# Gate and up weights of an expert in four transfers instead of two, in a hybrid decoder layer with 32 experts

## The reference

```python
def _hier_moe(x, w_r1, b_r1, w_r2, b_r2, w_gate, w_up, w_down):
    # top-1 of 4 groups, then top-2 of the 8 experts in the group; gate = p_group * p_expert
    ...
    for g in range(N_EXPERT_GROUPS):
        hg = jnp.einsum('nd,edf->nef', x, w_gate[g])
        hu = jnp.einsum('nd,edf->nef', x, w_up[g])
        a = jax.nn.silu(hg) * hu * gate[:, g, :, None].astype(x.dtype)
        y = y + jnp.einsum('nef,efd->nd', a, w_down[g]).astype(jnp.float32)
    return y.astype(x.dtype)
```

## Time and profile before

| | |
|---|---|
| median of three runs | 1018.94 us |
| profiled execution | 1017.82 us, of which span 1016.0 us |
| TensorE matmul busy | 906.7 us (89%) |
| TensorE weight load | 641.8 us (63%) |
| VectorE | 554.0 us (55%) |
| ScalarE | 409.7 us (40%) |
| GpSimd | 131.2 us (13%) |
| DMA, whole span | 273.49 MB, mean 269 GB/s |
| granted TensorE clock, mean | 0.958 |

### The profile page before, as it was taken

One profiled execution on the slowest core, in us unless ns is written; L12 is line 12 of the kernel. 1 busy time (PEld: TensorE's weight loads), 2 busy tenths in 40 slices (PEclk: granted clock), 3 DMA queues, 4 the chain that ended last, 5 costly groups with the idle time before them and its releaser, 6 DMA issues.

```text
span 1016.0 us, 13340 instructions
## 1 busy us (share of the span) xinstructions
PE 906.7 (89%) x5132; PEld 641.8 (63%) x5132; DVE 554.0 (55%) x1023; ACT 409.7 (40%) x748; POOL 131.2 (13%) x83
## 2 busy tenths in 40 slices
PE   6999999986999999759999826999999999999585
PEld 6999879953555545438888525666666666666231
DVE  5202020048566575683544476767676767666057
ACT  5202020034554644571222231564656555555045
POOL 0000000130000000000000002345464311111100
PEclk9999999988999999999999857999999999999888
DMA  9999999299587676418722373899999999995464
GB/s 349 310 366 357 353 346 345 76 395 251 184 319 246 232 249 208 166 36 322 248 83 68 135 325 104 308 366 362 369 350 358 350 373 354 366 355 198 161 254 167
DMA packets 54847, 273.49 MB, mean 269 GB/s; under 512 B 13984, under 2 KB 16544, under 8 KB 39680
## 3 DMA queue, kind: packets, MB, share of 16 engines
q1 hardware_dynamic: 46016, 247.97, 68.1%
q0 software_dynamic: 8768, 24.66, 6.9%
HBM read 256.33 MB, written 95.30 MB: 346 GB/s over the span
## 4 chain that ended last, share of the span: by engine, by line
PE 77%; DVE 10%; DMA 7%; issue 3%; ACT 3%; SPq 0%; POOLq 0%; DVEq 0%; ACTq 0%
PE psum L645 69%; DMA back<-w_gu 4%; PE psum L704 4%; PE psum L883 2%; DVE back L1231 1%; DMA back<-pair_d 1%; ACT back L490 1%; DVE back L1213 1%; DVE stats L1216 1%; PE psum L843 1%; ACT back L995 1%; DMA middle<-pair_d 1%; PE psum L906 1%; DVE middle L1241 1%; DVE middle L1590 0%
## 5 line engine op out<-in xcount | busy, mean ns | idle before, releaser
L645 PE MATMUL psum<-back,front 128*64 128x128 f32 (+1 forms) x896 | 147.9, 356 | 8.0 <-ACT back L490 4.4
L645 PEld LDWEIGHTS psum<-back,front 128*64 128x64 f32 (+1 forms) x896 | 69.4, 147 | 63.8 <-issue 54.3
L1656 POOL DMA_INDIRECT pair_d<-front,back x32 | 79.6, 2487 | 205.8 <-ACT front L1106 124.6
L645 PE MATMUL psum<-gu_high,xg_high 128*112 128x512 f32 x256 | 104.1, 407 | 2.1 <-DVE xg_low L1481 2.1
L645 PE MATMUL psum<-front 64*128 64x256 f32 (+5 forms) x384 | 92.6, 500 | 10.5 <-DVE stats L1213 9.9
L645 PE MATMUL psum<-gu_high,xg_low 128*112 128x512 f32 x256 | 101.8, 398 | 0.0
L645 PE MATMUL psum<-gu_low,xg_high 128*112 128x512 f32 x256 | 101.6, 397 | 0.0
L645 PE MATMUL psum<-x_high,w_high 128*128 128x352 f32 x288 | 93.7, 325 | 8.2 <-DVE w_low L361 8.2
L645 PE MATMUL psum<-x_low,w_high 128*128 128x352 f32 x288 | 93.0, 323 | 0.0
L645 PE MATMUL psum<-x_high,w_low 128*128 128x352 f32 x288 | 92.9, 322 | 0.0
L490 ACT COPY back<-psum 128x512 f32<-128x512 f32 (+1 forms) x88 | 46.9, 547 | 87.1 <-PE psum L704 86.9
(11 more groups left out here) (199 smaller groups left out, 1635.0 us busy)
## 6 DMA issues: line engine op xcount, KB each, us to landing
out_win_k_s<-cache_win_k SPq DMA_DIRECT2D x16, 2044.0 KB, 13.8
out_win_v_s<-cache_win_v SPq DMA_DIRECT2D x16, 2044.0 KB, 12.6
back<-w_down SPq DMA_DIRECT2D x24, 1024.0 KB, 14.7
front<-w_gu SPq DMA_DIRECT2D x22, 1024.0 KB, 12.7
middle<-w_gu SPq DMA_DIRECT2D x22, 1024.0 KB, 13.1
back<-w_gu SPq DMA_DIRECT2D x20, 1024.0 KB, 15.3
back<-winkT SPq DMA_DIRECT2D x8, 1792.0 KB, 8.0
back<-cache_win_v SPq DMA_DIRECT2D x8, 1024.0 KB, 7.5
```

The lines of the kernel that those rows point to most:

```text
L645: return nc.tensor.matmul(out, lhsT, rhs, start=start, stop=stop, skip_group_check=True)
L1656: G.indirect_dma_start(pair_d, bass.IndirectOffsetOnAxis(ap=IDX[0:CAP, NE + e:NE + e + 1], axis=0), YS[e % 2][0:CAP, :], None, bounds_chec ...
```

## The change

The gate and up weights of an expert are loaded in four transfers of 512 KB, two k-tiles each, in place of two of 1 MB. Each quarter has its own semaphore, ScalarE waits before each of its four casts, and TensorE signals `s_gu` after every second k-tile, so that SyncE is given back each quarter by itself. The other waits on `s_gu` count in quarters. Sizes and places of the buffers, the order on each engine and the bytes that are moved stay the same.

```diff
-        s_gf = [[sem(f"s_gf{i}_{h}") for h in range(2)] for i in range(3)]
+        s_gf = [[sem(f"s_gf{i}_{q}") for q in range(4)] for i in range(3)]
...
-        def load_gu(sp, e, half):
-            k = slice(4 * half, 4 * half + 4)
-            sp.dma_start(GUF[e % 3][:, k, :], I["w_gu"][e][:, k, :]).then_inc(s_gf[e % 3][half], 16)
+        def load_gu(sp, e, q):
+            k = slice(2 * q, 2 * q + 2)
+            sp.dma_start(GUF[e % 3][:, k, :], I["w_gu"][e][:, k, :]).then_inc(s_gf[e % 3][q], 16)
...
-            for half in range(2):
-                load_gu(sp, 0, half)
+            for q in range(4):
+                load_gu(sp, 0, q)
...
             for e in range(3, NE):
-                for half in range(2):
-                    sp.wait_ge(s_gu, 2 * (e - 3) + half + 1)
-                    load_gu(sp, e, half)
+                for q in range(4):
+                    sp.wait_ge(s_gu, 4 * (e - 3) + q + 1)
+                    load_gu(sp, e, q)
...
-                    if k % 4 == 3:
+                    if k % 2 == 1:
                         last.then_inc(s_gu, 1)
...
             def weights_rounded(e):
                 if e >= 2:
-                    act.wait_ge(s_gu, 2 * (e - 1))
+                    act.wait_ge(s_gu, 4 * (e - 1))
                 for q in range(4):
-                    if q % 2 == 0:
-                        act.wait_ge(s_gf[e % 3][q // 2], 16 * (e // 3 + 1))
+                    act.wait_ge(s_gf[e % 3][q], 16 * (e // 3 + 1))
                     k = slice(2 * q, 2 * q + 2)
                     nc.scalar.copy(GUH[e % 2][:, k, :], GUF[e % 3][:, k, :]).then_inc(s_wh, 1)
```

More of the change, by code:

```diff
@@ L613, in _ @@
                 sp.nop()
-            sp.wait_ge(s_gu, 2 * NE)
+            sp.wait_ge(s_gu, 4 * NE)
             for v, n in (("ln2_g", 0), ("ln2_b", 1)):
@@ L1096, in silu @@
             def silu(e):
-                act.wait_ge(s_gu, 2 * e + 2)
+                act.wait_ge(s_gu, 4 * e + 4)
                 if e >= 2:
```

## The result

The changed kernel takes 1027.79 us (median of 4 runs, 1026.17 to 1032.24) against 1018.67 for the kernel before in the same comparison: a ratio of 1.0093, 95% interval 1.0067 to 1.0119. It is slower by 9 us; 1019.4 was forecast with a range up to 1022.8, so the prediction failed, on the side of the "slower" rival and beyond its price of 3.6 us.

A forecast was written before the change was run, and what follows sets the result against it. Late in the expert loop the DMA engines' byte rate was taken to bound the kernel. 0 - 0.95 + 0 + 1.35 = +0.4 us on the median of 1018.94 gave 1019.4 us, range 1016.0 to 1022.8.

The forecast's parts named there:

- "slower" rival: DMA queue behind 655 us pays for packets and transfers: 0.17 us an expert, +3.6 us, time 1022.6; chance 0.18.
- What bounds the loop: Late in the expert loop, bytes a microsecond the DMA engines move set the limit; late weights cost 5.1 us.
- The queue is never empty: From about 655 us on the DMA queue always holds work, share 0.96 to 0.99 up to 820 us.
- Earlier requests: Quarters asked for sooner in the expert loop, expert 0's first by 2.7 us: taken as 0, bound 1.4 us.
- Earlier casts: On ScalarE, one cast instead of two after the last landing, so TensorE's down product comes sooner: -0.95 us, won once.
- Waits and hand-backs: Two added waits and hand-backs an expert, with more SyncE issues and TensorE signals, are hidden in the loop: 0.
- The price of shorter packets: Weight loads in 4 KB instead of 8 KB packets: +0.05 us an expert, +1.35 us over 27 experts.
- The far bound: Upper bound on the packet price, from a 410 GB/s row at 15 to 20 us: +0.17 an expert, +4.6 us.
- a bound on the fast side: Loop runs some 14% under loads alone; if shorter packets interleave better, up to the whole 5.1 us could go.
- The fit of 2.0 us a DMA: Skill's fixed time for each DMA; prediction said 424 GB/s back-to-back loads disagree with it per queued transfer, excluded it.
- "Faster": In the loop's mixed traffic, quarters beside 4 KB gather rows run better, all stalls go: 1013.8; chance 0.13.

The follow-up runs named there:

- experiment 9: ScalarE scales its output half before rounding the next weights: 0.9982 on the kernel before, 1.0041 on the changed kernel, 0.9990 on the kernel before with unbroken reads.
- experiment 8: Kernel before with one 2 MB transfer an expert in 16 KB packets, handed back whole and awaited ahead of the first cast: 1.0080.
- experiment 5: Changed kernel, but SyncE asks for two quarters at once when a half is free: 1.0063, and 1.0068 when run again beside the change.
- experiments 5 and 7: 7: weights laid out in DRAM for unbroken reads; changed kernel quarter by quarter 1.0064, kernel before half by half 1.0010.
- experiment 4: Kernel before with each 1 MB half issued as two 512 KB transfers, even and odd partitions, packets still 8 KB: 1.0003.
- Experiment 1: Kernel before with a 256 B gap after every 4 KB of weights in DRAM, so 1 MB transfers go in 4 KB packets: 1.0058.
- experiment 3: Kernel before with each 1 MB half issued as two 512 KB transfers, partitions 0 to 63 and 64 to 127, packets still 8 KB: 1.1857.
- the repeated change: The changed kernel, unaltered, timed once more against the kernel before: 1.0073.
- those with one queue: Gathers and scatters replaced by plain 112-row transfers in SyncE's weight queue: 1.0433 on the kernel before, 1.0468 on the changed kernel.

## Why the prediction was wrong, step by step

*What bounds the loop.* Right in the main: when the loads land. The new stalls and the later landings say so, and moving ScalarE's work (experiment 9) closes little of the gap. "The queue is never empty" held for the kernel before and for the changed one (share 0.98 to 0.99), not for coarser requests (experiment 8).

*Earlier requests, taken as 0.* Right as far as the runs can tell. The first quarter goes 2.4 us earlier, counted from the loop's start (628.93 - 626.00 = 2.9 us against 5.3):

```profile
628.93 5.73 SPq L468 DMA_DIRECT2D front<-w_gu  x4
```

and experiment 5 finds no gain in asking for quarters. In 640 to 660 us the DMA engines moved 299 GB/s, where it was 321 before, so no gain shows there.

*Earlier casts, -0.95 us.* The step is shorter by that much, 1.9 us from the last landing to the down product against 2.8, where that landing stops TensorE. That it took 0.95 us off the time is not shown: 1 MB transfers of 4 KB packets, without the earlier casts, measured 1.0058, and the kernels with them 1.0063 to 1.0093 (experiments 5 and 7, and the change itself).

*Waits and hand-backs, 0.* Right, within 2 us or so, for the number of transfers (experiment 4) and the hand-back (experiment 5). The waits ahead of single casts were never alone; nothing in the rows gives them a price.

*The price of shorter packets, 0.05 us an expert.* This is the step that failed. Measured are 0.23 us (6.8 us over 29 experts; 0.21 to 0.33 by neighbouring experts). Over the prediction's 27 experts that is 6.2 us where it had 1.35. Experiment 1, in which the packets alone were changed, cost 5.9 us (3.7 to 8.2). The far bound, 0.17, was too low as well.

A part of the error is where the price was read. Of the stretches of the earlier trace rows in which loads have the engines to themselves, the two with 4 KB packets are 3 us long. The first loads of the changed kernel, at 590 to 600 us, are a longer stretch of this kind:

```profile
590.00:600.00 10.00, 0.00 (x0) 0.00 (x0) 8.98 (x26) 0.23 (x1) 0.00 (x0) 0.50 1.02 412
```

412 against 424 GB/s are 2.8% less, where I had read 0.7 to 1.4% from the short ones. The other kernels with GpSimd's queue bear it out in the same ten microseconds: 411 to 417 GB/s with 4 KB packets, 402 with 2 KB, 418 to 426 with 8 and 16 KB (experiment 3 apart). At 412 GB/s an expert's 2.097 MB take 5.09 us, 0.144 more than at 424, and 27 of them 3.9 us; at the 417 of the repeated change it is 2.2 us. So the rate of loads alone accounts for a third to two thirds of experiment 1's loss.

The rest arises in the loop, and not where the traffic is merely mixed. These are the two queues in 660 to 780 us (packets, MB, share of the 16 engines), first of the kernel before, then of the changed one; q1 carries the weights, q0 the gathers and scatters:

```profile
q1 hardware_dynamic: 5091, 37.06, 84.6%
q0 software_dynamic: 3044, 6.08, 14.2%
```

```profile
q1 hardware_dynamic: 8399, 36.92, 84.8%
q0 software_dynamic: 3058, 6.11, 14.3%
```

and the same in 780 to 900 us:

```profile
q1 hardware_dynamic: 5050, 36.80, 83.0%
q0 software_dynamic: 3018, 6.62, 15.4%
```

```profile
q1 hardware_dynamic: 8075, 35.30, 82.0%
q0 software_dynamic: 2841, 6.41, 15.5%
```

MB by busy time of all engines, the early stretch: the weights 37.06 / (0.846 x 120) = 0.365 MB/us before and 0.363 after, the gathers and scatters 0.357 and 0.356. There is next to no difference. In the late stretch it is 0.369 and 0.359 for the weights, 3% less, and 0.358 and 0.345 for the gathers and scatters, though their packets are the same in both kernels. The kernel of experiment 4, with 8 KB packets and no loss, has 0.365 and 0.349 there, so most of the second difference can be scatter between profiles.

Over all profiles it is the same picture. From 660 to 780 us the kernels with 8 KB packets (again experiment 3 apart, and those with one queue) move 358 to 362 GB/s, those with 4 KB 357 to 361, that with 2 KB 355. From 780 to 900 it is 359 to 365, 344 to 358 and 342. The gap opens where TensorE begins to wait for late weights: in 780 to 800 us the two kernels still move 352 and 353 GB/s, in 800 to 820, with TensorE's first wait at 804.27 in the changed one, 362 and 335. The loads are asked for as TensorE frees their buffers, so a waiting TensorE also changes when transfers meet. Whether the rate falls first or TensorE's waits make it fall, no run tells apart. Nor does the rate account for everything: the last cast of expert 18 starts 4.8 us later in the changed kernel (802.38 - 626.00 against 795.86 - 624.29) while the windows up to 800 us are equal.

I had seen that the loop runs 14% under the rate of loads alone and used it only as a bound on the fast side, as if a loss that exists could only shrink.

The Trainium skill, "DMA: Bandwidth & Descriptors", Rules for kernel authors, asks for at least 1 MiB a DMA. The direction is that of this case, but the size of the transfer is not what counts here: 512 KB transfers with 8 KB packets measured 1.0003, and 1 MB transfers with 4 KB packets 1.0058. The Trainium skill's advice in the same table, that two transfers to disjoint partition halves are no use, fits the even and odd partitions (1.0003); for lower and upper halves it is weak, as the runs show a loss of 19% of the whole kernel. The fit of 2.0 us a DMA that the prediction took from the Trainium skill, "DMA: Bandwidth & Descriptors", Anatomy of one DMA, is stated there for transfers issued by GpSimd; the weight loads are SyncE's, so their 424 GB/s neither confirm nor refute it.

*The rivals.* "Slower" had the loss in the loads' queue right and, at 0.17 us an expert, the price too small. "Faster" is excluded: no stretch of the loop got clearly faster. The chance of 0.18 for slower was too low for a price read from stretches unlike the one in question.

**What stays open.** By what mechanism 4 KB packets cost more in the late loop than alone. Not by the order in DRAM or the number of transfers, and, as far as one pair of profiles goes, not by the software queue. The changed kernel shows a pattern: its scalings of an output come in pairs, at 825.71, 834.05, 846.99, 855.35, 868.03, 876.99, 889.69, steps of 8.3 to 9.0 and of 12.7 to 12.9 us in turn, where the kernel before had steps of 10.3 to 10.9. TensorE then waits before every second down product. The loss does not need it: the repeated change, the same kernel, waits before one down product after another up to 857 us, in steps of 10.4 to 11.3 us, and only then falls into pairs. At 855.55 us, the last cast of expert 23, it is already 5.9 us late of the 6.9 at the end.

```profile
826.64 3.66 PE L645 MATMUL psum<-back,front 128*112 128x512 f32 x8 [2.24 <-ACT front L1105]
847.93 3.66 PE L645 MATMUL psum<-front 128*112 128x512 f32 x8 [1.11 <-ACT front L1105]
```

```profile
835.98 3.66 PE L645 MATMUL psum<-back,front 128*112 128x512 f32 x8 [0.80 <-ACT front L1105]
846.52 3.66 PE L645 MATMUL psum<-front 128*112 128x512 f32 x8 [0.32 <-ACT front L1105]
857.44 3.66 PE L645 MATMUL psum<-back,front 128*112 128x512 f32 x8 [0.74 <-ACT front L1105]
```

## What to carry to other kernels

A packet size has no one price that could be carried from stretch to stretch. Here 4 KB in place of 8 KB cost 0.7 to 1.4% of the rate in windows of 3 us and 1.7 to 3% in windows of 10, both with loads alone; 0.3% in mixed traffic while the loads had a lead, and 4% where TensorE waited for them. The cheap and sure test is experiment 1: change the packets alone and time it. Splitting a transfer into even and odd partitions, with each partition's run kept whole, was free; splitting along the run was not, and splitting into lower and upper partitions was far worse. And a step that gets shorter once, by 0.95 us, weighs little against a price that every expert pays.

## What the runs showed that I had not expected

Two transfers of 64 partitions each, partitions 0 to 63 and 64 to 127, move 224 GB/s with the engines busy at 0.98; the same bytes by even and odd partitions move 359. The kernel is 19% slower by the one and unchanged by the other.

A single 2 MB transfer an expert, in 16 KB packets, is 0.8% slower than two of 1 MB, with the engines idle for 4% of the late loop where it was 1%.
